# Two transformer blocks in one launch: weight splits, turns and an affine step rearranged where one block hands over to the next

## The reference

```
first_block:   x = x + gate * token_mixers(modulate(rmsnorm(x)))        # gated recurrent and spatial mixing
               h2 = modulate(rmsnorm(x, g_ffn), mod[3], mod[4])
               x = x + gate * swiglu(h2, w_up, w_down)
               return rmsnorm(x, g_final)
second_block, for each of two layers:
    f = swiglu_2(rms_norm(x, g[0]), ...);  x = x + 0.5 * rms_norm(f, g[1])
    m = attention(rms_norm(x, g[2]), ...); x = x + rms_norm(m, g[3])     # stick-breaking, then latent attention
    f = swiglu_2(rms_norm(x, g[4]), ...);  x = x + 0.5 * rms_norm(f, g[5])
swiglu_2(x):   gate, up = split(x @ w_in);  (silu(gate) * up) @ w_out
```

## Time and profile before

| what | value |
|---|---|
| median of three runs | 1502.95 us (1502.86 to 1503.41) |
| the profiled execution | 1502.86 us |
| its span in the trace | 1501.6 us |
| PE busy | 1448.4 us, 96% |
| DVE busy | 857.9 us, 57% |
| ACT busy | 752.0 us, 50% |
| granted TensorE clock, mean | 0.985 of full speed |
| weights and other reads | 265 MB, 177 GB/s |

### The profile page before, as it was taken

How to read it: one execution, slowest core, us unless ns; L and a number is a source line. 1 busy time by engine, 2 the same in 40 slices (tenths; PEclk the granted TensorE clock), 3 DMA queues, 4 the chain that set the end, 5 groups by cost and what they waited for, 6 DMA issues and landing times.

```text
span 1501.6 us, 19638 instructions
## 1 busy us (share of the span) xinstructions
PE 1448.4 (96%) x8098; PEld 1213.2 (81%) x8098; DVE 857.9 (57%) x1187; ACT 752.0 (50%) x1078; POOL 22.4 (1%) x72
## 2 busy tenths in 40 slices
PE   6899999989999999999999999999999999899998
PEld 4899689868888788888898788887888888788886
DVE  3636675685554665556454755657555465665543
ACT  3325353554454455544565654446545475555442
POOL 0000000000000000000021000000000000000000
PEclk8999899999999999999999999999999999999999
DMA  9237467545555565555533556555555551355552
GB/s 383 87 116 291 158 226 252 183 140 180 183 183 192 172 202 186 188 184 195 182 113 100 187 185 188 186 192 187 184 187 189 182 176 57 113 161 185 187 184 97
DMA packets 69930, 267.34 MB, mean 178 GB/s; under 512 B 7760, under 2 KB 8016, under 8 KB 66384
## 3 DMA queue, kind: packets, MB, share of 16 engines
q1 hardware_dynamic: 67680, 259.13, 51.6%
q10 hardware_dynamic: 2160, 6.95, 1.4%
HBM read 265.00 MB, written 1.05 MB: 177 GB/s over the span
## 4 chain that ended last, share of the span: by engine, by line
PE 87%; DVE 8%; ACT 3%; issue 1%; DMA 0%; SPq 0%; POOL 0%; DVEq 0%; ACTq 0%
PE PS L720 22%; PE PS L736 13%; PE PS L738 13%; PE PS L737 13%; PE PS L371 4%; PE PS L372 4%; PE PS L373 4%; DVE WL L1619 2%; PE PS L704 2%; PE PS L468 1%; PE PS L403 1%; PE PS L404 1%; PE PS L405 1%; DVE TN L2034 1%; PE PS L439 1%
## 5 line engine op out<-in xcount | busy, mean ns | idle before, releaser
L1619 DVE TENSOR_TENSOR WL<-RAW,WH 128x1024 fp32r<-128x1024 f32 (+1 forms) x440 | 531.7, 1220 | 332.9 <-ACT WH L1085 332.4
L1085 ACT ACTIVATE WH<-RAW 128x1024 fp32r<-128x1024 f32 (+1 forms) x440 | 453.7, 1054 | 293.8 <-DMA RAW<-in_up 172.4
L736 PE MATMUL PS<-WH,XH 128*128 128x512 f32 (+1 forms) x928 | 383.0, 413 | 14.3 <-DVE XL L2042 14.1
L738 PE MATMUL PS<-WH,XL 128*128 128x512 f32 (+1 forms) x928 | 363.8, 392 | 0.0
L737 PE MATMUL PS<-WL,XH 128*128 128x512 f32 (+1 forms) x928 | 363.6, 392 | 0.0
L736 PEld LDWEIGHTS PS<-WH,XH 128*128 128x128 f32 x928 | 175.4, 189 | 64.8 <-DVE XL L2042 19.2
L738 PEld LDWEIGHTS PS<-WH,XL 128*128 128x128 f32 x928 | 175.5, 189 | 37.5
L737 PEld LDWEIGHTS PS<-WL,XH 128*128 128x128 f32 x928 | 176.3, 190 | 28.1
L720 PE MATMUL PS<-WH,GH 128*128 128x512 f32 x440 | 137.4, 393 | 0.0
L720 PE MATMUL PS<-WL,GH 128*128 128x512 f32 x440 | 135.7, 390 | 0.0
L720 PE MATMUL PS<-WH,GL 128*128 128x512 f32 x440 | 135.7, 389 | 0.0
(11 more groups left out here) (343 smaller groups left out, 1832.1 us busy)
## 6 DMA issues: line engine op xcount, KB each, us to landing
RAW<-in_up SPq DMA_DIRECT2D x220, 512.0 KB, 4.7
RAW<-in_down SPq DMA_DIRECT2D x110, 512.0 KB, 3.3
RAW<-in_win SPq DMA_DIRECT2D x44, 512.0 KB, 6.4
RAW<-in_mod SPq DMA_DIRECT2D x16, 1024.0 KB, 6.7
MC<-in_mod SPq DMA_DIRECT2D x8, 1024.0 KB, 14.2
RAW<-in_sbqk SPq DMA_DIRECT2D x16, 512.0 KB, 4.7
GROW<-in_grow ACTq DMA_DIRECT2D x9, 512.0 KB, 4.2
RAW<-in_wo SPq DMA_DIRECT2D x8, 512.0 KB, 4.1
```

What stands on the lines that cost most here:

```text
L736: e.matmul(o_[:, 0:n], l, w[:, s], start=(k == 0), stop=False, skip_group_check=True)
L738: m = e.matmul(o_[:, 0:n], ll, w[:, s], start=False, stop=(k == KD - 1), skip_group_check=True)
L1085: e.activation(WH[s][:, 0:c], RAW[s][:, 0:c], ACT.Copy).then_inc(*sig("hi", j))
L1619: e.tensor_tensor(WL[s][:, 0:c], RAW[s][:, 0:c], WH[s][:, 0:c].bitcast(F32), ALU.subtract).then_inc(*sig("lo", j))
```

## The change

It does five things, all at the boundaries:

- On TensorE the turn of half 1 is issued in two pieces: quarter 0 after step 3 of half 0, quarter 1 after step 4 of half 0. In block 5 the second piece comes right behind the first, since that block has no step 4.
- On VectorE the order for half 1 becomes scale, XL, scale, XL; before it was scale, scale, XL, XL.
- Chunk 5 is split behind the XH and XL of half 1 on ScalarE and VectorE, and no longer ahead of them. Chunk 6 is left to the loop of the coming block, at p = 3.
- For b < 2 the adds to X follow the products at once. So the XL of half 0, quarter 1, comes behind the adds of half 1.
- For b = 0 the eight 128-column instructions with two scalars per partition become, for each quarter, one product and one in-place sum of 512 columns with broadcast operands; ScalarE waits for a new signal `tm`, and the sum waits for the product.

```diff
--- before.py
+++ after.py
@@ -746,9 +746,8 @@
                 for p in range(n + LAG):
                     if p < n:
                         step(p, 0)
-                    if came is not None and p == LAG - 1:
-                        turn(came, 1, 0)
-                        turn(came, 1, 1)
+                    if came is not None and LAG - 1 <= p <= LAG:
+                        turn(came, 1, p - LAG + 1)
                     if p >= LAG:
                         step(p - LAG, 1)
                     if left is not None and p >= n + LAG - 2:
@@ -998,9 +997,8 @@
             for p in range(8):
                 if p < 4:
                     mla_step(p, 0)
-                if p == 3:
-                    turn(5, 1, 0)
-                    turn(5, 1, 1)
+                if 3 <= p <= 4:
+                    turn(5, 1, p - 3)
                 if p == 7:
                     latents_turned(0)
                 if p >= 4:
@@ -1323,7 +1321,7 @@
 
             def turned(b, h, z):
 
-                ac.wait_ge(*at("tn", b, h, z))
+                ac.wait_ge(*(at("tn", b, h, z) if b else at("tm", h, z)))
                 e.activation(XH[:, 4 * z:4 * z + 4, h * P:(h + 1) * P], four(TN.of(("tn", b, h, z))[:, :]),
                              ACT.Copy).then_inc(*sig("xh", b, h, z))
 
@@ -1349,11 +1347,11 @@
                 square_of(b, 1, 1)
                 root(b, 1)
                 if b < 7:
-                    split(c0 + 6)
                     if b:
                         scale_of_input(b, 0)
                     turned(b, 1, 0)
                     turned(b, 1, 1)
+                    split(c0 + 5)
                     if b:
                         scale_of_input(b, 1)
                 ac.wait_ge(*at("x", b, 1, 1))
@@ -1981,9 +1979,6 @@
                         dv.wait_ge(*at("sq", b, h, 0))
                     e.tensor_tensor(y[:, :], BANK.of(banks[n])[:, :], grow[:, n * 512:(n + 1) * 512],
                                     ALU.mult).then_inc(*sig("y", b, h, n))
-
-            def added(b, h):
-
                 if b < 2:
                     dv.wait_ge(s_x, 16)
                     for n in (1, 0):
@@ -2026,14 +2021,13 @@
                 dv.wait_ge(*after(before))
                 if b == 0:
                     dv.wait_ge(*at("dve", "vf"))
-                    for k in range(k0, k0 + 4):
-                        c = slice((k - k0) * P, (k - k0 + 1) * P)
-                        m = e.tensor_scalar(tn[:, c], BANK.of(("xt", b, h, z))[:, c], VEC[:, 40 + k:41 + k],
-                                            MOD[:, 24 + k, 0:1], ALU.mult, ALU.add)
-                else:
-                    m = e.tensor_tensor(four(tn[:, :]), four(BANK.of(("xt", b, h, z))[:, :]),
-                                        bc(G2(*BEFORE[b], k0, 4), P), ALU.mult)
-                m.then_inc(*sig("tn", b, h, z))
+                g = VEC[:, 40 + k0:44 + k0] if b == 0 else G2(*BEFORE[b], k0, 4)
+                e.tensor_tensor(four(tn[:, :]), four(BANK.of(("xt", b, h, z))[:, :]), bc(g, P),
+                                ALU.mult).then_inc(*sig("tn", b, h, z))
+                if b == 0:
+                    dv.wait_ge(*at("tn", b, h, z))
+                    e.tensor_tensor(four(tn[:, :]), four(tn[:, :]), bc(MOD[:, 24 + k0:28 + k0, 0], P),
+                                    ALU.add).then_inc(*sig("tm", h, z))
 
             def turned(b, h, z):
 
@@ -2048,7 +2042,6 @@
 
             def boundary(b, c0):
                 updates(b, 0)
-                added(b, 0)
                 sum_of(b, 0)
                 inverse(b, 0)
                 renewed(b, 0, 0)
@@ -2061,7 +2054,6 @@
                 updates(b, 1)
                 if b < 7:
                     turned(b, 0, 1)
-                added(b, 1)
                 sum_of(b, 1)
                 if b < 7:
                     split(c0 + 4)
@@ -2069,14 +2061,13 @@
                 renewed(b, 1, 0)
                 renewed(b, 1, 1)
                 if b < 7:
-                    split(c0 + 5)
                     if b:
                         scale_of_input(b, 0)
                     scaled(b, 1, 0)
+                    turned(b, 1, 0)
                     scaled(b, 1, 1)
-                    turned(b, 1, 0)
                     turned(b, 1, 1)
-                    split(c0 + 6)
+                    split(c0 + 5)
                     if b:
                         scale_of_input(b, 1)
```

## The result

The changed kernel takes **1523.99 us** (median of 4 runs, 1522.97 to 1528.6) against 1503.03 (1502.86 to 1503.41): ratio **1.0151, 95% interval 1.0128 to 1.0174**, so it is slower by 21 us; 1522.3 was predicted. The profiled execution took 1525.93 us, with a span of 1524.7.

The account below looks back on a forecast made before the run. TensorE was taken as the bound, 87% of the chain and busy 96% of the span. Losses 12.8 + 2.7 + 0.7 + 1.2 = 17.4, with the clock 19.4, on 1502.86 gave 1522.3 us; range 1512 to 1531.

Parts of the forecast that it names:

- Chunk 5 late by t+4.22: With t the first XL's start, TensorE starts step 5 of half 0 at t+4.22; at boundary 4, +1.97 us.
- chunk 6 by t+6.50+I: Step 6 starts at t+6.50+I, I running from second square to table load; boundaries 2, 3, 4, 6 lose 12.8 us.
- The table load without a drain behind it: On ScalarE the table load holds 1.30 us; the skill's 1.38 us drain, some 8 us more, is left out.
- Boundary 1: XL of half 1 gains 1.5 us, but step 6 comes at 532.49 instead of 529.77: +2.7 us.
- The interleaving costs nothing: VectorE's TN, XL, TN, XL leaves the first XL's start unchanged: gain zero at boundaries 2, 3, 4 and 6.
- t+1.32: Start of the second XH on ScalarE, 1.32 us after the first XL, 0.73 after the second TN begins.
- Boundary 5: Second square behind chunk 5's WH delays the latents' turn from 1222.49 to 1223.2: +1.2 us, between 0 and 2.
- The clock: New TensorE waits bring half-clock stretches of 3.5 us, each up to 1.7 us: 2 us taken, bounds 0 and 10.2.
- boundary 0: Step 0 of half 1 comes at 331.7 instead of 332.40, but chunk 6 lets step 6 go at 338.9: +0.7 us.
- The two-piece turn, the adds and the broadcast pair cost nothing: Turn in pieces: cost zero; boundary 0's product and sum: 1.41 us against 1.36; moved adds delay boundary 1's turn, 521.08 to 521.31.
- The faster rival: XL gains at boundaries 0, 1, 5 stand alone if both moved chunks come in time: 1500.2 us; 5%.
- waits announced on WL: TensorE waits before step 5 (about 2 us) and step 6 (1.1 to 2.2 us) per boundary, 12 in all.

Follow-up runs that it names:

- e3: The changed kernel with chunk 6 split at the boundary again, right behind chunk 5 on both engines; 1521.51 us, ratio 1.0112.
- e7: The changed kernel with ten unused matmuls in TensorE's wait ahead of the latents' transposes at boundary 5; 1526.24 us, ratio 1.0141.
- e6: The kernel before with only VectorE's order for half 1 changed to TN, XL, TN, XL; 1502.49 us, ratio 0.9993.
- e2: The kernel before with only the splits of chunks 5 and 6 moved as in the change; 1507.28 us, ratio 1.0033.
- e5: The kernel before with the moved splits and VectorE's order TN, XL, TN, XL; 1524.28 us, ratio 1.0119.
- e1: The changed kernel with only the splits of chunks 5 and 6 put back to their old places on both engines; 1501.62 us, ratio 0.9986.
- e4: The kernel before with chunk 5's WH behind X's first square, its WL between the XLs, chunk 6 behind the second XH and XL; 1500.35 us, ratio 0.9984.
- e8: The kernel e4 with chunk 6 of boundary 5 left to the attention's own split; 1497.53 us, ratio 0.9955.
- e10: The same kernel as e8, timed again beside e9; 1498.46 us, ratio 0.9957.
- e9: The same kernel as e4, timed again on one chip beside e10; 1500.42 us, ratio 0.9977.

## Why the prediction was right, and where it was not

- **Chunk 5 late by t+4.22, chunk 6 by t+6.50+I: right.** At boundary 4 both instants are met within 0.03 us, and stages 2, 3 and 4 lose 3.20, 3.83 and 3.36 us against 3.1, 3.6 and 3.1. e3 separates the two: without chunk 6 behind the table load 1.1 to 1.3 us come back. e7, the same code there, repeats the three stages within 0.02 us.
- **The table load without a drain behind it: right.** 1042.21 plus 1.28 is 1043.49, and WH starts at 1043.51. The drain of about 1.38 us that the Trainium skill gives (page "ScalarE: Activation LUTs", section "What ACT_TABLE_LOAD costs") is not seen here either.
- **Boundary 1: right in sum, with two errors that nearly cancel.** The loss was 2.68 against 2.7. XL came 0.35 us later than worked out and the table load 0.64 sooner after the square (2.02 instead of 2.66).
- **The interleaving costs nothing: the number was right, the attribution wrong.** "Gain zero" holds in e6. But the prediction booked all of the loss to the moved splits, and in stages 2 to 4 these alone (e2) lose 5.9 us of the 10.4. The 0.73+0.66 us by which the second XH comes later stood in my formula, in t+1.32, under another heading. Whoever had taken the prediction's headings as a guide to what to undo would have undone more than needed.
- **Boundary 5: the wait was right, the stage not.** The latents' transposes start 17.12 us into the stage where it was 16.39, +0.73, as worked out (1222.49 to 1223.2). Behind them the changed kernel ran at half clock. e5 has the same splits and the same wait, at clock 1.00, and its stage 5 is +1.09, where 1.2 was predicted. So some 4.4 of the +5.47 are clock.
- **The clock: the step that was mis-sized.** I took 2 us. The boundaries together lost 25.5 us in the profiled run. The waits take about 18.4 of them, against 17.4 predicted: stages 0 and 1 of e7 (+0.79 and +2.39), stages 2 to 4, and stages 5 and 6 of e5 (+1.09 and +3.72, the last still with some low clock). That leaves about 7 us for the clock, within the bounds of 0 and 10.2, but not where I had placed them. My argument was that a stretch at half clock between the two new waits would hide in the second. At boundary 1 it did: 529.00 to 532.50 had a clock of 0.51, and step 6 started at 532.26, when its weight was there. At boundary 0 it did not. The changed kernel's VectorE and TensorE:

```profile
334.86 1.23 DVE L1617 TENSOR_TENSOR WL<-RAW,WH 128x1024 fp32r<-128x1024 f32 x1 [1.15 <-ACT WH L1083]
```

```profile
333.76 0.50 PE L736 MATMUL PS<-WH,XH 128*128 128x512 f32 x1 [2.56 <-DVE WL L1617]
...
338.21 0.40 PE L736 MATMUL PS<-WH,XH 128*128 128x512 f32 x1
```

  WL of chunk 6 is ready at 336.09, but TensorE needs 4.45 us for the twelve matmuls from 333.76 on and comes at 338.21, 2.1 us after it. Against before (step 6 at 338.2, in a stage that began 2.36 us later) that is the +2.37. e7 has no fall there:

```profile
336.70 0.50 PE L736 MATMUL PS<-WH,XH 128*128 128x512 f32 x1 [2.54 <-DVE WL L1624]
...
339.56 0.39 PE L736 MATMUL PS<-WH,XH 128*128 128x512 f32 x1
```

  It needs 2.86 us for the twelve, and the stage is +0.79 where +0.7 was predicted. The number was right by luck: the prediction let chunk 6 set step 6 there, but its weight is ready ahead of TensorE in e7 too, and chunk 5's delay decides alone. At boundary 6, 1.24 of the +4.55 lie ahead of half 1's turn, where the change has moved nothing, in a stretch at 0.50. These losses are met in part by the opening: 2.36 us less in code that no edit touches, by luck of the clock. So the closeness of 1522.3 to 1524 owes something to two clock effects of opposite sign; the median of all 21 executions is 3 us further off.
- **The two-piece turn, the adds and the broadcast pair cost nothing: right within the noise.** e1 has all of them at 1501.62 against 1503.06. The product and the in-place sum behind it took 1.42 us for a quarter, as the rows below show; 1.41 was taken.

```profile
326.71 0.69 DVE L2025 TENSOR_TENSOR TN<-PS,VEC 128x512 f32<-128x512 f32 x1 [1.42 <-PE PS L694]
327.44 0.69 DVE L2029 TENSOR_TENSOR TN<-TN,MOD 128x512 f32<-128x512 f32 x1
...
328.83 0.69 DVE L2036 TENSOR_TENSOR XL<-TN,XH 128x512 fp32r<-128x512 f32 x1 [0.69 <-ACT XH L1325]
```

- **The faster rival** needed both chunks in time. e4 and e8 have that, and are faster; its condition, not its mechanism, was what the change missed. Of the waits announced on WL ten were there, not twelve: at boundaries 0 and 1 TensorE reached step 6 when its weight was there already.

Open: what sets the moment of the clock's fall, and how much of the 21 us the clock takes in the mean of many runs (the changed kernel itself has one profiled execution here).

## To carry to other kernels

When work is moved behind a chain that goes to and fro between two engines, add up what the receiving engine waits inside the chain, not only what it does: 1.36 us of idle ScalarE, free until then, became part of the path at five boundaries, and 2.08 us at boundary 0. An edit that costs nothing alone (-0.7 us) and one that costs 9.4 can cost 17.1 together, so try each alone and both together before one is blamed, and compare stage by stage: by the medians the two looked like -1.0 and +4.2. And when an early operation holds up a late one in one place, move it just behind the one it holds up rather than to the end of the queue (e8, 0.9955).

## What the runs showed of the hardware

- **The granted clock differs between executions of one program,** and the time with it: the changed kernel's executions, those run beside the experiments among them, ran from 1518.85 us at a mean clock of 0.988 to 1528.77 at 0.979, some 1.1 us for 0.001 of clock. The kernel before ran from 1497.3 to 1509.33. In the opening the code is the same in all kernels, yet the stretch took 317.5 us in before, 315.1 in the changed kernel, 312.3 in e8 and 317.8 in e10, which is e8's kernel. Even with 12 runs against 23, e9's interval is 0.0029 wide, 4.4 us; a smaller difference is better read in stages where both had the full clock.
- **Half clock can last while TensorE is busy:** in the two windows of e7 above, TensorE was busy in all of 10 us and was granted 0.50 of full speed throughout.

- **Stages without a fall repeat almost to the instruction:** each of the stages 2 to 4 of e4, e6 and e8 is within 0.4 us of the same stage of before, and within 0.03 for e4, e8, e9 and e10, whose code works in time there. Such a stage resolves a wait that the total does not. Stage 3 of the changed kernel, then of before, both at clock 1.00:

```profile
835.20:1027.48 192.28, 188.43 (x853) 153.13 (x852) 113.20 (x147) 98.32 (x137) 0.00 (x0) 1.00 0.57 184
```

```profile
829.31:1017.76 188.45, 187.66 (x853) 153.18 (x852) 113.22 (x147) 98.42 (x137) 0.00 (x0) 1.00 0.59 188
```

TensorE does the same 853 instructions; its idle time grew from 0.79 to 3.85 us, 3.06 of the 3.83. The other 0.77 is busy time at the same clock. About 0.27 of it comes with each of the two new waits, by the rows of boundary 4: the matmul ahead of a wait counts its full 0.39 us, where the next one would have started after 0.23, and from the first one behind a wait the next starts after 0.34 instead of 0.23. The last 0.2 stays open.
